# Streaming encoder step on one core: state stores on SyncE, and VectorE's output normalisation ahead of the level differences

## What is computed

```python
proj = einsum('btd,dn->btn', h, w_in)            # q, forget, value, output gate, conv pair, gates
logf = log_sigmoid(zf) + log1p(lb * exp(-zf));  k = (1 - lb) * sigmoid(-zf)
def gla_block(S, q, k, v, logf):                 # one block of a head
    b = cumsum(logf)
    attn = einsum('td,sd,tsd->ts', q, k, exp(b_t - b_s) * causal)
    o = attn @ v + (q * exp(b)) @ S
    S_new = exp(b_last) * S + (k * exp(b_last - b)).T @ v
    return S_new, o
o = rms_norm(o, hg_norm_g) * silu(g_o)           # per head
y_a = o @ w_o_a
```

## Time and profile before

| | |
|---|---|
| median of 3 runs | 864.47 us |
| the profiled execution | 866.9 us, its span 865.0 us |
| mean granted TensorE clock | 0.981 |
| TensorE busy | 812.2 us (94%) |
| VectorE busy | 426.4 us (49%) |
| ScalarE busy | 236.6 us (27%) |
| POOL busy | 31.7 us (4%) |
| DMA | 251.16 MB, mean 290 GB/s |

### The profile page before, as it was taken

The page is one execution under the profiler, slowest core; times in us unless marked ns, Lnnn a source line. Parts: engine busy times, 40 slices in busy tenths (PEclk is TensorE's granted clock), DMA queues, the critical chain, the costliest instruction groups (busy, mean ns, idle before and its releaser), DMA issues.

```text
span 865.0 us, 12835 instructions
## 1 busy us (share of the span) xinstructions
PE 812.2 (94%) x5092; PEld 525.3 (61%) x5092; DVE 426.4 (49%) x714; ACT 236.6 (27%) x362; POOL 31.7 (4%) x42
## 2 busy tenths in 40 slices
PE   4888989999999999999999999999999999999892
PEld 2888888889999976677553353533535335352351
DVE  6788888988999994786110211202112020120127
ACT  6555556656446426102012000000000001000011
POOL 1011111111000010000000000000000000000000
PEclk9999989999999999998999999999999999999997
DMA  8422222323544762578999999999999999999991
GB/s 315 165 80 67 99 82 81 110 105 104 174 143 145 288 247 64 227 292 345 406 392 396 427 428 427 424 429 426 425 429 427 424 428 429 427 423 429 430 389 66
DMA packets 33882, 251.16 MB, mean 290 GB/s; under 512 B 4974, under 2 KB 8430, under 8 KB 21674
## 3 DMA queue, kind: packets, MB, share of 16 engines
q1 hardware_dynamic: 31296, 249.18, 71.2%
q10 hardware_dynamic: 2538, 1.32, 0.5%
HBM read 247.99 MB, written 2.48 MB: 290 GB/s over the span
## 4 chain that ended last, share of the span: by engine, by line
PE 60%; DVE 22%; DMA 8%; ACT 7%; issue 2%; ACTq 0%; DVEq 0%
PE ps L559 58%; DMA ring<-in_w_up_e 8%; DVE ar L1781 6%; DVE ring L1659 4%; DVE split_t L1788 3%; ACT ring L1235 1%; DVE ar L1695 1%; PE ps L966 1%; ACT ar L1245 1%; DVE ar L1650 1%; DVE ar L1706 1%; ACT split_w L1156 1%; ACT ar L1209 1%; DVE ring L1569 1%; DVE ar L1702 1%
## 5 line engine op out<-in xcount | busy, mean ns | idle before, releaser
L559 PE MATMUL ps<-ring,ar 128*64 128x512 f32 (+1 forms) x976 | 202.0, 567 | 1.3 <-DMA ring<-in_w_up_e 1.2
L559 PE MATMUL ps<-ring,xT 128*64 128x512 f32 (+2 forms) x848 | 141.8, 451 | 4.6 <-DMA ring<-in_w_gate_e 3.0
L559 PEld LDWEIGHTS ps<-ring,ar 128*64 128x64 f32 x976 | 68.0, 137 | 120.6 <-issue 111.8
L559 PEld LDWEIGHTS ps<-ring,xT 128*64 128x64 f32 (+1 forms) x848 | 68.3, 153 | 70.8 <-issue 62.6
L559 PE MATMUL ps<-split_x,split_t 128*128 128x320 f32 x672 | 101.0, 310 | 0.5 <-DVE split_t L1788 0.5
L559 PEld LDWEIGHTS ps<-split_x,split_t 128*128 128x128 f32 x672 | 98.6, 188 | 2.3 <-issue 0.8
L2091 DVE TENSOR_TENSOR ar<-ar,ps 128x512 f32<-128x512 f32 (+1 forms) x42 | 28.8, 685 | 134.9 <-PE ps L559 133.1
L559 PE MATMUL ps<-split_x,split_w 128*128 128x320 f32 x480 | 85.0, 336 | 6.1 <-DVE split_w L1620 3.5
L559 PEld LDWEIGHTS ps<-split_x,split_w 128*128 128x128 f32 x480 | 78.5, 207 | 10.2 <-DVE split_w L1620 3.9
L559 PE MATMUL ps<-ar 128*64 128x512 f32 (+5 forms) x424 | 65.7, 345 | 11.0 <-DVE mid L1724 11.0
L1781 DVE SCALAR_TENSOR_TENSOR ar<-ar,params 128x350 f32<-128x350 f32 x116 | 68.7, 592 | 4.1
(11 more groups left out here) (233 smaller groups left out, 821.9 us busy)
## 6 DMA issues: line engine op xcount, KB each, us to landing
ring<-in_w_gate_e SPq DMA_DIRECT2D x29, 2048.0 KB, 21.3
ring<-in_w_up_e SPq DMA_DIRECT2D x29, 2048.0 KB, 18.1
ring<-in_w_down_e SPq DMA_DIRECT2D x22, 2048.0 KB, 17.6
ring<-in_w_in SPq DMA_DIRECT2D x56, 512.0 KB, 4.5
ar<-in_w_down_e SPq DMA_DIRECT2D x4, 1792.0 KB, 19.0
ring<-in_w_down_end SPq DMA_DIRECT2D x3, 2048.0 KB, 36.8
ar<-in_w_up_e SPq DMA_DIRECT2D x3, 1792.0 KB, 14.6
ring<-in_w_o_a SPq DMA_DIRECT2D x8, 512.0 KB, 5.6
```

What stands on the lines that cost most here:

```text
L559: return pe.matmul(out, lhsT, rhs, start=start, stop=stop)
```

## The change

Two edits. `store_states` leaves ScalarE's program; SP stores the states of head n-2 in its loop, between its wait for `so_ready` n-1 and the wait for `o_done`, and those of heads 6 and 7 behind the loop, each behind a wait for `so_ready`. And in VectorE's turn `pprev_out` stands ahead of `level_decay`.

```diff
@@ sync
+            def store_states(n):
+                for s, name in enumerate(("new_hgrn_prompt", "new_hgrn_sample")):
+                    sp.dma_start(o[name][0, 0, bass.ds(n, 1)].rearrange("o p n -> (o p) n"), hSo[:, s, :]).then_inc(h["so_stored"], 16)
...
                     sp.wait_ge(h["v_done"], 2 * i + b - 1)
                     load_head(i, b)
                     sp.wait_ge(h["so_ready"], 2 * i + b - 1)
+                    store_states(2 * i + b - 2)
                     sp.wait_ge(h["o_done"], 2 * i + b - 1)
                     load_state(i, b)
             for b in range(2):
                 sp.wait_ge(h["v_done"], 7 + b)
                 load_u(2 * b)
                 load_u(2 * b + 1)
+                if b == 0:
+                    sp.wait_ge(h["so_ready"], 7)
+                    store_states(6)
             for b in range(2):
                 sp.wait_ge(ulo_ready, 4 * b + 4)
+                if b == 1:
+                    sp.wait_ge(h["so_ready"], 8)
+                    store_states(7)
                 load_pair(b, (G0 // P + 2 * b, G0 // P + 2 * b + 1))
@@ scalar
-            def store_states(i, b):
-                n = 2 * i + b
-                act.wait_ge(h["so_ready"], n + 1)
-                for s, name in enumerate(("new_hgrn_prompt", "new_hgrn_sample")):
-                    act.dma_start(o[name][0, 0, bass.ds(n, 1)].rearrange("o p n -> (o p) n"), hSo[:, s, :]).then_inc(h["so_stored"], 16)
...
                     prev_square(*prev, first_prev)
-                    store_states(*prev)
...
             prev_square(3, 1, False)
-            store_states(3, 1)
@@ vector
                     level_fold(*prev)
-                level_decay(*cur)
                 if pprev:
                     pprev_out(*pprev)
+                level_decay(*cur)
                 if nxt:
                     w_low(*nxt, 0)
```

## The result

The changed kernel took **860.05 us** (median of 8 runs, 857.88 to 862.02) beside 864.67 for the kernel before (8 runs). The ratio is 0.9942, with a 95% interval of 0.9926 to 0.9958: faster by 0.6%, so by more than the 0.2% that can be told. The profiled execution took 860.37 (span 858.5, mean granted clock 0.987); the one of before had a span of 865.0 at 0.981.

What follows compares the result with a forecast made beforehand. Head turns were taken as a loop of waits with ScalarE mostly last and VectorE the next bound. Turn gains less 0.58 in the tail summed to 3.9 us; 3.4 off 864.47 gave 861.0, range 858.9 to 864.5.

Steps and rivals of the forecast that it cites:

- Part 1: Stores moved to SP: 0.92 us leaves ScalarE's chain per head; SP's later loads taken at nothing, bounds 0 and 0.5.
- the signs that the prediction had named as wrong: Hole where ScalarE's issues were, new L1156 or L1672 wait over 0.5, other turns' clock 0.50, or unchanged end despite gain.
- Part 2's step 2: TensorE's output matmuls no longer wait for L1724: start 1.44 earlier in turn 6; turn 4's forget projection 1.1 earlier.
- the upper of its two values: Opening of turn 5: gain 2.11 (the cap) if the clock stays up, 1.1 if it falls; 1.6 taken.
- VectorE's sum is unchanged: Head turns: moving L1724 ahead of the seven L1659 leaves VectorE's total work the same.
- step 1: ScalarE's exponential L1235 and whole chain start 0.58 later (0.55 and a gap); L1672 loses at most 0.1.
- the time from L1706 to L1235: Sign in the head turns: this time grows by 0.6.
- the rms matmuls of the tail: Sign in the tail: rms stands 3.4 to 4.4 before 189.40.
- That the issue costs nothing: Rival: hole before L1203 has another cause than the stores, so part 2 acts alone; 864.5, chance 0.11.
- That the DMA stream hides the gain: Rival: the expert weight stream, not its triggers, sets the end; some 0.5 is left, 864.0, chance 0.05.
- Slower by the clock: Rival: TensorE's idle time ahead of the forget projection lowers the clock, projection 5.62 each turn; +2.7, 867.2, chance 0.06.
- more: Rival: clock stays up, every cap reached; 0.5 more in turn 5, 0.2 in turn 4; 858.9, chance 0.08.

Runs made afterwards that it cites:

- filled kernel: Kernel before, plus four matmuls with unread result ahead of the output matmuls in each turn from 2 on; ratio 0.9992, 863.23 us beside 864.25.
- norm ahead of the fold: Changed kernel with `pprev_out` moved one step further forward, ahead of the `level_fold` that starts POOL's level sums; ratio 0.9981, 862.27 us.
- stores alone: Kernel before with only the state stores moved from ScalarE to SP, `pprev_out` staying behind `level_decay`; ratio 0.9966, 860.9 us beside 863.35.
- POOL later: Kernel before with an added wait holding POOL's level sums until the turn's level differences are done; 882.67 us, single run, beside 864.25.
- normalisation only: Kernel before with only `pprev_out` moved ahead of `level_decay`, the stores staying on ScalarE; ratio 1.0017, 865.21 us.

## Why the prediction was right

Forecast was 861.0 (858.9 to 864.5), measured 860.05; the median is 0.95 lower than forecast and in the range. The sign, the places and the mechanism held; one term was mis-sized, and the profile shows it more than the median does: the profiled execution took 860.37 where 863.0 was forecast. The nearness of the median is in part luck, since the 0.5 taken off for executions without the fall in turn 4 was a guess; the medians moved by 4.6 where 3.4 was forecast. By its steps, each against the profile of before (the opening of turn 2 gains what turn 1 is shorter, 20.57 − 19.71 = 0.86, and so on):

| opening of | forecast | measured | last in the turn, after |
|---|---|---|---|
| turn 2 | 1.07 | 0.86 | ScalarE |
| turn 3 | 0.64 | 0.96 | VectorE |
| turn 4 | 0.5 | 0.67 | ScalarE |
| turn 5 | 1.6 | 2.43 | VectorE |
| turn 6 | 0.3 | 0.64 | ScalarE |
| turn 7 | 0.34 | 0.62 | ScalarE |
| tail | −0.58 | −0.22 | ScalarE |
| together | 3.9 | 5.96 | |

**Part 1** went nearly as written. ScalarE goes from square to gate in 0.03 in turn 6, but in 0.26 in turn 1 and in 0.52 in turn 3. That 0.26 is why turn 2 gave 1.12 − 0.26 = 0.86 and not 1.07. SP's weight loads start 0.1 to 1.1 later within their turns (0.9 was forecast). In turn 2 one landed late, and ScalarE's copy waited 0.60 for it, which is one of the signs that the prediction had named as wrong (over 0.5). It was covered all the same: ScalarE idles 5.02 right ahead of that turn's exponential.

```profile
68.51 1.07 ACT L1167 ACTIVATE split_w<-ring 128x1024 fp32r<-128x1024 f32 x1 [0.60 <-DMA ring<-in_w_in]
```

**Part 2's step 2** held as well: the output matmuls wait for nothing in any turn, and of the gap of 2.56 in turn 4 one of 1.21 is left, now ahead of the forget projection:

```profile
118.33 3.79 PE L570 MATMUL ps<-split_x,split_w 128*128 128x320 f32 x24 [1.21 <-DVE split_w L1623]
```

I had forecast 2.1 there and left open whether the clock would fall. The gap is shorter because the split comes 0.40 sooner in its turn (the table below) and TensorE's own work before it 0.6 later. The clock stayed up and the projection took 3.79: turn 5 got the upper of its two values. By the filled kernel 1.69 (22.46 − 20.77) of its 2.43 are the clock of that one profile.

**What was mis-sized** is one assumption under part 2, "VectorE's sum is unchanged", and with it the 0.58 of step 1 ("L1235 starts 0.58 later"). The start of VectorE's next weight split and of ScalarE's exponential, in us behind the L1643 (L1646) of the same turn:

| | turn 2 | 3 | 4 | 5 | 6 | 7 (tail) |
|---|---|---|---|---|---|---|
| split, before | 11.56 | 11.49 | 11.55 | 11.48 | 10.72 | 10.74 |
| split, after | 11.16 | 11.01 | 11.15 | 11.00 | 10.44 | 10.37 |
| split, norm ahead of the fold | 11.55 | 11.50 | 11.55 | 11.48 | 10.73 | 10.74 |
| exponential, before | 10.81 | 10.70 | 10.79 | 10.69 | 10.19 | 10.21 |
| exponential, after | 11.11 | 10.93 | 11.10 | 10.92 | 10.50 | 10.43 |
| exponential, norm ahead of the fold | 11.50 | 11.42 | 11.50 | 11.41 | 10.79 | 10.80 |

VectorE is through the same work 0.28 to 0.48 sooner, since the seven differences take 4.26 to 4.46 instead of 4.75, and ScalarE's exponential is only 0.22 to 0.31 later, not 0.58. Where ScalarE is last, the forecast was short by the difference: 0.97 − 0.31 − 0.03 = 0.63 for turn 7 (measured 0.62), and in the tail 0.22 is lost instead of 0.58. Where VectorE is last, it lifts the cap: 0.69 + 0.40 for turn 3 and 2.16 + 0.40 for turn 5 are what its shorter work allows, 0.96 and 2.43 were measured; some 0.13 of either went elsewhere, where I had allowed 0.05. With the normalisation ahead of the fold the split is back at the old times and the exponential is 0.59 to 0.72 later; its turn 6 gains 19.82 − 19.49 = 0.33, which is the 0.34 that I forecast for the opening of turn 7.

So two of the prediction's signs failed: the time from L1706 to L1235 grew by half of the 0.6, and the rms matmuls of the tail stand 5.80 before 189.40 and not 3.4 to 4.4.

I could have seen it: in the kernel before the seven take 3.66 in turn 0, where POOL has nothing to do, and 4.74 or more in all turns where it has. The mean of the group hides that.

**The rivals.** That the issue costs nothing falls by the closed hole and by the stores alone (0.34%). That the DMA stream hides the gain falls by 4.2 us carried to the experts. Slower by the clock falls: the gaps right ahead of the forget projection are there in turns 2 to 5, 0.63 to 1.21 us, and no turn from 2 to 6 had a fall in either profile; the tail fell in one of the two. The rival "more" (858.9) was missed by 1.15, on the other side; what it said of turn 5 came true and was exceeded, and turn 4 got 0.17 of its 0.2, though for another reason than it gave: VectorE's shorter work.

## What to carry to other kernels

Moving a short step can pay by what it puts beside another engine: look which VectorE operations with both inputs in SBUF run while GpSimd works, compare their time in a turn where it doesn't, and put an operation that reads PSUM in that place. Two parts of a change that each relieve a different engine can be worth little or nothing alone where the engines are nearly level (here 0.34% and −0.17%, together 0.58%), so a part is to be judged on top of the other. And where a loop of waits is nearly level, every turn's gain is capped by the next engine's own work, which has to be measured and not assumed constant.

## What the runs showed of the hardware

**VectorE and POOL take turns.** Seven `tensor_tensor` of SBUF operands took 3.66 us alone and 4.75 with all four of POOL's sums beside them; POOL's first sum took 1.00 alone and 1.15 to 1.16. The single instructions of turn 6 show who waited for whom. In the kernel before (the difference that starts at 157.01 is the second of the seven; POOL's first sum is the 156.67 1.16 shown above):

```profile
157.01 1.17 DVE L1659 TENSOR_TENSOR ring<-ar 128x320 f32<-128x320 f32 x1
157.91 0.59 POOL L1531 TENSOR_TENSOR ar<-ar 64x128 f32<-64x128 f32 x1
158.21 0.63 DVE L1659 TENSOR_TENSOR ring<-ar 128x320 f32<-128x320 f32 x1
```

Then the first of the seven in the changed kernel, and one with POOL idle (POOL later, turn 2):

```profile
151.74 0.82 DVE L1662 TENSOR_TENSOR ring<-ar 128x256 f32<-128x256 f32 x1
```
```profile
75.62 0.49 DVE L1661 TENSOR_TENSOR ring<-ar 128x320 f32<-128x320 f32 x1
```

A difference of 320 columns takes 0.49 alone. One that starts while a sum of POOL runs ends 0.35 behind that sum: POOL's first ends at 157.83, the difference at 158.18; POOL's second at 158.49, the next at 158.84. POOL's sums wait in the same way: the second starts at 157.91 and ends 0.32 behind the difference that ran when it started. So each was held until the other's instruction was through. That is also where the change gains. Before, POOL's first sum held a difference of 320 columns for 0.68 us (1.17 − 0.49) and was itself held for 0.16; now it starts beside the normalisation, takes its 1.00, and holds only the short first difference of 256 columns, 0.82 instead of 0.42.

The Trainium skill (SBUF — State Buffer, Who interferes with whom) says that a VectorE instruction with two inputs in SBUF contends with a GpSimd instruction that reads SBUF, and one with at most one such input, outside the modes that use two ports, does not. The trace agrees with both halves: the normalisation, which has one input in PSUM, takes 0.55 beside POOL and leaves it its 1.00. The Trainium skill (SBUF — State Buffer, SBUF: two separate sides) says that whichever of two such instructions starts first keeps the shared ports for its whole length, and the other blocks. The trace agrees with that too, by the 0.35 above, which is the same within 0.01 for every such 320-column difference of turns 2 to 6, in both kernels.

**The clock does not follow from the length of the gap alone.** Ahead of turn 1 the changed kernel's TensorE stood idle 2.18 us in one profile and 2.54 in the other, before the same matmuls; the clock fell to 1.2 GHz behind the shorter one and stayed at 2.4 behind the longer. The two profiles, with the wait, the stretch behind it and the L1646 that opens turn 1 (2.0 us apart, of which 0.5 was there before), the one that fell first:

```profile
37.47 5.76 PE L570 MATMUL ps<-split_x,split_w 128*128 128x320 f32 x27 [2.18 <-DVE split_w L1623]
...
38.00:40.00 2.00, 2.00 (x9) 2.00 (x9) 1.90 (x4) 1.87 (x5) 0.00 (x0) 0.50 1.04 395
...
45.67 0.49 DVE L1646 SCALAR_TENSOR_TENSOR ar<-ps,ar 128x320 f32<-128x320 f32 x1 [2.04 <-ACT ar L1220]
```
```profile
36.99 6.28 PE L570 MATMUL ps<-split_x,split_w 128*128 128x320 f32 x41 [2.54 <-DVE split_w L1623]
...
38.00:40.00 2.00, 2.00 (x15) 2.00 (x15) 1.86 (x5) 1.86 (x5) 0.00 (x0) 1.00 0.89 320
...
43.67 0.49 DVE L1646 SCALAR_TENSOR_TENSOR ar<-ps,ar 128x320 f32<-128x320 f32 x1 [0.50 <-ACT ar L1220]
```

The 1.41 in the tail fell in one of these two profiles and held in the other. In turns 2 to 6 of all profiles gaps up to 1.67 brought no fall; 1.73 (normalisation only, turn 2), 2.11, 2.37, 2.49, 2.56 and all of POOL later (2.43 to 3.28) did, and 2.04 (normalisation only, turn 4) did not. In the tail of the filled kernel a fall followed a gap of 0.67. What decides it was not found. A single profile of such a kernel (POOL later apart) has none to three of these falls before 200 us, not counting its first 30; those that could be priced cost 0.6 to 1.7 us each, as much as a part of the change.
